# Reordering the first pairs of each feed-forward stage in a two-layer decoder step: the first seven-product pair's silu and product ahead of the plain pair's, and the copy of up and a weight split ahead of the last token group

## The reference

```python
def swiglu(h, w_gate, w_up, w_down):
    return (jax.nn.silu(h @ w_gate) * (h @ w_up)) @ w_down

for i in range(DEPTH):
    xp = xp + 0.5 * swiglu(rmsnorm(xp, ffn_norm[i, 0]), ffn_w_gate[i, 0], ffn_w_up[i, 0], ffn_w_down[i, 0])
    ...
    xp = xp + yp        # yp: sparse attention in layer 0, sliding window attention in layer 1
    ...
    xp = xp + 0.5 * swiglu(rmsnorm(xp, ffn_norm[i, 1]), ffn_w_gate[i, 1], ffn_w_up[i, 1], ffn_w_down[i, 1])
```

## Time and profile before

| | us |
|---|---|
| median of 3 runs | 2277.26 |
| lowest and highest | 2271.42, 2283.96 |
| time of the profiled execution | 2277.23 |
| its span, first to last instruction | 2275.4 |
| TensorE busy | 2154.5 |
| VectorE busy | 1334.2 |
| GpSimd busy | 1174.3 |
| ScalarE busy | 947.3 |

### The profile page before, as it was taken

How to read it: one execution, slowest core, us unless ns; L and a number is a source line. 1 busy time by engine, 2 the same in 40 slices (tenths; PEclk the granted TensorE clock), 3 DMA queues, 4 the chain that set the end, 5 groups by cost and what they waited for, 6 DMA issues and landing times.

```text
span 2275.4 us, 40915 instructions
## 1 busy us (share of the span) xinstructions
PE 2154.5 (95%) x15007; PEld 1969.7 (87%) x15007; DVE 1334.2 (59%) x2282; ACT 947.3 (42%) x1891; POOL 1174.3 (52%) x817
## 2 busy tenths in 40 slices
PE   7799999999989889899999899999999998999997
PEld 6799999958766578899999899999997698999997
DVE  5736455778885448637365753637556567455453
ACT  5425344341454325525255442525314435344343
POOL 4638576414201027748575775848641067666571
PEclk9899999999998999999999999999999898999998
DMA  5344453644203442444444252444461033535341
GB/s 129 71 114 106 121 112 93 118 80 121 41 2 101 123 103 56 90 87 91 87 93 93 66 102 65 97 91 91 96 152 31 1 75 67 111 69 117 66 103 42
DMA packets 378147, 197.68 MB, mean 87 GB/s; under 512 B 66531, under 2 KB 374476, under 8 KB 377932
## 3 DMA queue, kind: packets, MB, share of 16 engines
q1 hardware_dynamic: 366108, 180.79, 35.9%
q10 hardware_dynamic: 11552, 13.71, 2.0%
q0 software_dynamic: 288, 0.56, 0.1%
HBM read 192.23 MB, written 11.64 MB: 90 GB/s over the span
## 4 chain that ended last, share of the span: by engine, by line
PE 51%; DVE 6%; ACT 2%; issue 2%; POOL 2%; DVEq 0%; POOLq 0%; ACTq 0%
PE psum L1054 8%; PE psum L1055 8%; PE psum L1056 8%; PE psum L1013 7%; PE psum L1014 4%; PE psum L1016 4%; PE psum L1012 4%; PE psum L1015 3%; DVE squares L2495 1%; DVE psum L2347 1%; PE psum L1386 1%; PE psum L1416 1%; PE psum L1402 1%; PE psum L1382 1%; DVE XS L2336 1%
## 5 line engine op out<-in xcount | busy, mean ns | idle before, releaser
L802 POOL CAST WSP<-WST 128x1024 fp32r<-128x1024 f32 (+1 forms) x41 | 45.0, 1098 | 486.5 <-PE psum L1016 339.0
L835 POOL TENSOR_TENSOR WSP<-WST,WSP 128x512 fp32r<-128x512 f32 x106 | 153.4, 1451 | 151.3 <-ACT WSP L1739 151.2
L1054 PE MATMUL psum<-XT,WSP 128*128 128x288 f32 x656 | 199.2, 304 | 8.7 <-ACT back_up L1770 7.3
L1055 PE MATMUL psum<-XT,WSP 128*128 128x288 f32 x656 | 197.0, 300 | 0.0
L1056 PE MATMUL psum<-XT,WSP 128*128 128x288 f32 x656 | 196.2, 299 | 0.0
L1054 PE MATMUL psum<-XS,WSP 128*128 128x288 f32 x552 | 165.0, 299 | 15.9 <-DVE GS L2422 15.9
L2595 DVE SCALAR_TENSOR_TENSOR X<-psum,X 128x576 f32<-128x576 f32 x64 | 48.4, 756 | 213.6 <-PE psum L1016 213.6
L1056 PE MATMUL psum<-XS,WSP 128*128 128x288 f32 x552 | 163.5, 296 | 0.0
L1055 PE MATMUL psum<-XS,WSP 128*128 128x288 f32 x552 | 163.5, 296 | 0.0
L1013 PE MATMUL psum<-GS,WSP 128*128 128x512 f32 x406 | 161.5, 398 | 0.0
L2347 DVE SCALAR_TENSOR_TENSOR psum<-S,WST 128x512 f32<-128x512 f32 x70 | 107.2, 1531 | 86.3 <-POOL S L815 84.8
(11 more groups left out here) (450 smaller groups left out, 7454.6 us busy)
## 6 DMA issues: line engine op xcount, KB each, us to landing
WST<-in_ffn_w_gate SPq DMA_DIRECT2D x148, 256.0 KB, 4.8
WST<-in_ffn_w_down SPq DMA_DIRECT2D x144, 224.0 KB, 4.2
WST<-in_ffn_w_up SPq DMA_DIRECT2D x104, 256.0 KB, 4.1
WSTX<-in_ffn_w_up SPq DMA_DIRECT2D x64, 256.0 KB, 4.3
WSTX<-in_ffn_w_down SPq DMA_DIRECT2D x48, 224.0 KB, 4.2
WST<-in_a_w_in SPq DMA_DIRECT2D x28, 256.0 KB, 4.5
kv0A<-in_cache_kv SPq DMA_DIRECT2D x48, 128.0 KB, 2.3
kv2A<-in_cache_kv SPq DMA_DIRECT2D x48, 128.0 KB, 2.3
```

What stands on the lines that cost most here:

```text
L835: nc.gpsimd.tensor_tensor(by_pair(low), raw, by_pair(high).bitcast(F32), ALU.subtract).then_inc(pool_set, 1)
L1054: mm(out, high[:, c], operand(prod, 0, k), start=first and k == 0, stop=False, skip_group_check=True)
L1055: mm(out, high[:, c], operand(prod, 1, k), start=False, stop=False, skip_group_check=True)
```

## The change

On DVE and ACT the plain pair's last steps move behind the first seven-product pair's. In ffn1 to ffn3 that is: DVE runs the hidden chain of pair 1 and the gate of pair 2, then the plain pair's four operations, and only then `up_second(2)`. In ffn0 with its two plain pairs, plain pair 0 is finished after the gate of pair 3 and plain pair 1 after the gate of pair 4. The numbers that the semaphores count to follow (`hidden_before`). ACT's silus and high copies move alike.

At the head of ffn1 to ffn3, ACT copies the plain pair's up product (`up_copy`) before the high parts of the last token group's first sum and of P6's and P3's weights. POOL makes the low part of P5's weights before `last_sum(i, 2)` and P2's, and the tokens' low parts ahead of the sum S3. In ffn0, DVE takes the plain gate ahead of the last token sums.

```diff
+def hidden_before(name, p):
+
+    order = [PLAIN[name]]
+    for k in range(PLAIN[name]):
+        order += [k, PLAIN[name] + 1 + k]
+    return FFNS.index(name) * NF + (order.index(p) if p in order else p)
...
@@ GpSimd, start @@
+                if i:
+                    first_sum(i, 2)
+                    sum_up(name, p)
+                    low_of_raw(name, p, "P1")
+                    token_low(i, 2, 0)
+                    low_of_sum(name, p, "P5")
+                    last_sum(i, 2)
+                    low_of_raw(name, p, "P2")
+                    first_sum(i, 3)
+                    token_low(i, 2, 1)
+                    token_low(i, 3, 0)
+                    sum_first(name, p)
+                    last_sum(i, 3)
+                    token_low(i, 3, 1)
...
@@ TensorE, p1 @@
                 if p > 1 and plain(name, p - 2):
                     pe.wait_ge(gate_set, 2 * (n - 1))
+                elif p > 1:
+                    pe.wait_ge(hidden_set, 2 * (hidden_before(name, p - 2) + 1))
...
@@ ScalarE, update @@
                         scaled(6)
                         scaled(7)
+                        up_copy(to, PLAIN[to] - 1)
                         token_high(3, (0,))
                         high_of(to, PLAIN[to], "P6")
                         high_of(to, PLAIN[to], "P3")
-                        up_copy(to, PLAIN[to] - 1)
                         token_high(3, (1, 2, 3))
...
@@ ScalarE, ffn @@
+                    silu(name, p)
                     if q == 0:
-                        for k in range(p):
-                            silu(name, k)
-                    silu(name, p)
+                        silu(name, 0)
...
-                        if q == 0 and p == first + 1:
-                            for k in range(first):
-                                hidden_high(name, k)
                         hidden_high(name, p - 1)
                         next_high(p, "P2")
                         next_high(p, "P7")
                         silu(name, p)
                         next_high(p, "P4")
+                        if q == 0 and plain(name, p - first - 1):
+                            hidden_high(name, p - first - 1)
+                            if plain(name, p - first):
+                                silu(name, p - first)
...
@@ VectorE, load_x @@
+                plain_gate("ffn0", 0)
                 token_sums(0, 3)
-                plain_gate("ffn0", 0)
...
@@ VectorE, ffn @@
-                        if q == 0 and p == first + 1:
-                            for k in range(first):
-                                plain_up(name, k)
-                                plain_hidden(name, k)
-                                plain_low(name, k)
                         hidden(name, p - 1)
                         hidden_low(name, p - 1)
                         gate_second(name, p)
                         gate_first(name, p)
                         gate_scaled(name, p)
+                        if q == 0 and plain(name, p - first - 1):
+                            plain_up(name, p - first - 1)
+                            plain_hidden(name, p - first - 1)
```

More of the change, by code:

```diff
@@ L236, in count_pool @@
                 if follows_plain(name, p):
-                    keys += [(name, p, k) for k in ("S1", "P1", "P2", "P5", "S3", "P7")]
+                    keys += [(name, p, k) for k in (("S1", "P1", "P5", "P2") if FFNS.index(name) else ("S1", "P1", "P2", "P5"))]
+                    keys += [(name, p, k) for k in ("S3", "P7")]
                 else:
@@ L533, in plain_room @@
         def plain_room(half, p):
+            if half == "up_back" and p:
+                half, p = "gate_back", 0
             return plain_rooms[half, p][:, :]
@@ L921, in start @@
                     token_low(i, 1, 1)
[L922 to L938, removed]
+                if i:
[12 more added lines that the diff above has]
+                    token_low(i, 3, 1)
+                else:
+                    for k in range(KP):
+                        first_sum(i, k)
+                        token_low(i, k, 0)
+                        last_sum(i, k)
+                        if k < 2:
+                            low_of_plain(name, 1, halves_of_plain(1)[k])
+                        elif k == 2:
+                            sum_up(name, p)
+                            low_of_raw(name, p, "P1")
+                            low_of_raw(name, p, "P2")
+                            low_of_sum(name, p, "P5")
+                            sum_first(name, p)
+                        token_low(i, k, 1)
                 low_of_sum(name, p, "P7")
@@ L1945, in hidden_high @@
             def hidden_high(name, p):
-                act.wait_ge(hidden_set, 2 * pair_number(name, p) + 1)
+                act.wait_ge(hidden_set, 2 * hidden_before(name, p) + 1)
                 fn(GH[:, p % DB, :], plain_room("up", p) if plain(name, p) else bank_ab(name, p), ACT.Copy).then_inc(gh_set, 1)
@@ L2409, in hidden @@
             def hidden(name, p):
-                n, ab = pair_number(name, p), bank_ab(name, p)
+                n, ab = hidden_before(name, p), bank_ab(name, p)
                 dve.wait_ge(w_used, DONE[name, p, "P4"])
-                dve.wait_ge(up_sum, n + 1)
+                dve.wait_ge(up_sum, pair_number(name, p) + 1)
                 steps.done(stt(ab, ab, -1.0, rstd[:, :], ALU.mult, ALU.mult))
@@ L2418, in hidden_low @@
             def hidden_low(name, p):
-                n = pair_number(name, p)
+                n = hidden_before(name, p)
                 dve.wait_ge(gh_set, n + 1)
@@ L2441, in plain_hidden @@
             def plain_hidden(name, p):
-                n, u = pair_number(name, p), plain_room("up", p)
+                n, u = hidden_before(name, p), plain_room("up", p)
                 dve.wait_ge(silu_done, n + 1)
                 tt(u, u, plain_room("gate", p), ALU.mult).then_inc(hidden_set, 1)
-            def plain_low(name, p):
-                n, u = pair_number(name, p), plain_room("up", p)
                 dve.wait_ge(hidden_set, 2 * n + 1)
```

## The result

The changed kernel takes 2286.39 us (median of 20 runs, 2280.24 to 2292.83), the kernel before 2275.30 us in the same comparison (20 runs). The ratio is 1.0047, 95% interval 1.0036 to 1.0057: slower by 11 us. The interval does not hold 1, so the difference is real, but it lies just under the 0.5% that the prediction took as the line between no change and slower. The profiled execution's span is 2285.2 us against 2275.4.

The account below looks back on a forecast made before the run. PE bounds the kernel, busy 95% of the span, the rest its waits. 3 x (2.7 + 0.4) for ffn1 to ffn3 plus 2.9 for ffn0 gives +12.2, 2289.5 us; own range 2283 to 2296, overall 2272 to 2300.

Parts of the forecast that it names:

- The exchange of stalls: ffn1: P1(3)'s wait mostly goes; P5(3) waits 5 to 7 us for `up_second`, with clock 0.50 behind it.
- the step: Tail, ffn1: hidden chain and P1(3) start 4.30 us earlier; plain operations meet POOL's backlog of four, P5(3) at 927.45.
- rival (c): POOL's backlog holds DVE 5.54 us, so P1(4) waits too; head takes its full bound: 2294 us, chance 0.12.
- The blocked port: Tail, ffn1: the plain pair's DVE operations are held beside POOL's, 1.3 to 2 us each; P5(3) at 927.4.
- Rival (a): Tail: DVE's later three plain operations are not held beside POOL; P5(3) at 924.5, sum -2.6, 2274.6 us, chance 0.20.
- The row that carried the estimate: L2347, a two-input DVE operation right behind a POOL operation: 0.69 us at least, 1.78 in the middle, 5.54 at worst.
- for the tail: Plain pair behind pair 1 in ffn1: P6(3) at 932.66 instead of 929.94, costing 2.7 us.
- the head's term: Head of ffn1: the wait moves from P5(1) to P6(1), 3.5 us; costs 0.4, bounds -0.1 and +1.0.
- 5.21 - 3.75: From P5(3) to P6(3): P5 and P4 take 3.16 us plus 2.05 for the slow clock.
- +2.9: ffn0: -0.4 - 0.8 + 6.1 - 2.05, from its head and two plain-pair insertions, with a new stall at P5(5).
- The head's term there: ffn0: earlier plain gate gains PE about 2 us at P1(2); waits for copies and weights leave a gain of 0.4.
- Rival (b): Clock stays at 2.4 GHz through new stalls at P6(1) and P5(3): -15.3, 2274.2 us ports blocked, 2259 free; chance 0.12.

Follow-up runs that it names:

- the tail part alone: Changed kernel with GpSimd's order, `up_copy` and ffn0's plain gate put back, leaving only the plain pair's later finish: 2284.05 us, 1.0043 of the kernel before.
- the head part alone: Kernel before with only GpSimd's order, `up_copy` and ffn0's plain gate as in the changed kernel: 2273.90 us, 1.0000 of the kernel before.
- the last experiment: Kernel before plus plain pair ahead of weight sums, its high copies later, new heads, and P1's product copy before P7's high part: 2256.36 us, 0.9922.
- the kernel with GpSimd held: Changed kernel, with GpSimd also waiting before P2's weights' low part until the plain pair's values are finished: 2277.09 us, 1.0013 of the kernel before.

## Why the prediction came out as it did

**The exchange of stalls held.** P1(3)'s wait went from 5.83 to 1.51 and P5(3) waits 6.21 behind `up_second`, with the clock at 0.50. P1(3) came 4.20 us earlier where 4.30 was the step (4.33 in the tail part alone, in ffn1), and from P1(3) to P5(3) it was 8.05 us against the 8.6 that was worked out. P1(4) did not wait, so rival (c), a further wait, fell. (Its sum was off as well: 3 x (0.8 + 0.6) is 4.2, not 4.5, which still ends at 2294.)

**The blocked port held, and decides.** Rival (a), a free port, asks for P5(3) at most 5.65 us behind P1(3). With GpSimd idle it is 5.46; with GpSimd beside it, as in the change, 8.05. The row that carried the estimate, L2347, was a fair guide: 0.69 to 1.78 there, 0.76 to 1.71 here. The Trainium skill, "SBUF — State Buffer", section "Who interferes with whom", says that a VectorE instruction with two SBUF inputs and a GpSimd instruction that reads SBUF contend. The trace agrees for the three plain operations that met one, 1.12, 1.71 and 1.70 us in place of 0.41, 0.76 and 0.76. The fourth took 0.76: GpSimd's backlog had run out by then, as the step had counted.

**In ffn1 the sum came out by two errors that cancel.** Up to P5(3) the prediction has 1.26 (927.45 - 926.19) for the tail and 0.4 for the head, +1.66 in each of three stages; measured were +0.81, +0.76 and +0.69, that is 2.7 us less in all. 0.55 us of it a stage lie between P1(3) and P5(3): the first plain operation started 1.45 us behind P1(3) instead of 1.67, and from there to `up_second` it was 6.09 instead of 6.43. The rest is the head's term and the little by which P1(3) was early. Behind P5(3) the prediction has 5.21 - 3.75 = 1.46 us in all three stages. From P5(3) to P6(3) it was 5.93 us in ffn1, 5.18 in ffn2 and 4.54 in ffn3, and before, that stretch took 3.75, 4.32 and 3.37. So the difference is 2.18, 0.86 and 1.17, which is 4.2 in all against 4.4: right in the sum and in no single stage. ffn1's +3.08 against 3.1 is 0.85 too little before P5(3) and 0.72 too much behind it, and that is luck. ffn1 was copied to the other two stages on the strength of a like pattern of waits; the clock behind them was not alike. The three stages cost 6.6 us instead of 9.3, nearly all of it before P5(3), and that is most of the gap between the forecast of 12.2 and the 9.8 of the profiled spans. The medians differ by 11.1, with an interval of about 8 to 13, which holds both 9.8 and 12.2.

**The head.** Its term of +0.4 is nothing that can be measured: the head part alone gives 1.0000 [0.9991, 1.0009]. The wait moved to P6(1), as said, and was 3.42 against 3.5. Its releaser was another one. In the changed kernel, ScalarE's timeline shows

```profile
901.28 0.61 ACT L1767 ACTIVATE WSP<-S 128x512 fp32r<-128x512 f32 x1
901.80 0.39 ACT L1950 ACTIVATE shots<-psum 128x288 f32<-128x288 f32 x1
```

and GpSimd's low part, which the prediction named, is done before:

```profile
900.86 0.80 POOL L890 TENSOR_TENSOR XT<-tsum,XT 128x288 fp32r<-128x288 f32 x1
```

It ends at 901.66, ScalarE's copy at 902.19, and P6(1) starts at 902.25. P6(1) also needs ScalarE's copy of P1's product, which the list of waits ahead of the prediction leaves out too. That copy's place behind L1767 makes half a microsecond of the wait: with it ahead of L1767 in the last experiment, the stall was 2.96.

**ffn0.** +2.8 measured against +2.9, with stalls at P5(4) and, new, at P5(5), 5.64 us behind P1(5) against 5.7. The head's term there had the wrong sign: it was a gain of 0.4, but counted from the end of the plain part, P1(4) starts at 27.39 us in the changed kernel and at 27.01 in the tail part alone. What P1(2) gains by its 2.37 us goes into longer waits for ScalarE's copies, 1.47 us at P6(2), where there was none, and 1.85 at P6(3), where there was 0.72.

**The clock does not stay up.** Rival (b) fell for the long stalls: 0.50 to 0.65 in the stretches behind the stalls of about 6 us, and 0.50 over 4.4 us behind the 3.61 at P5(3) of the kernel with GpSimd held. For stalls of 3.4 us it is true in some stages and not in others; the last section has the numbers. Most of (b)'s chance stood under faster, though with the port blocked its own time, 2274.2, is no change.

What stays open: the kernel with GpSimd held has 10.4 us less of waits behind `up_second`, and its ratio is 0.0034, about 8 us, better than the changed kernel's. The two ratios are to different sets of runs, and each interval reaches about 2.5 us to either side, so the two figures do not contradict each other, and the contention's price in the median is known no more closely. The spread of single runs of the changed kernel, 2280 to 2293, is as wide as the effect. The longer ones tend to have the lower mean granted clock: the correlation is -0.63 over its 20 runs, and between -0.41 and -0.82 in each set of runs of the experiments. Which stalls lower the clock in one run and not in another was not tested.

## What to carry to other kernels

Work that is moved out from under one wait in an in-order queue lands on the next: list for each engine it runs on who stands behind it now and when that one is needed, ScalarE's hop included. Look for the place by the moved engine's own idle time ahead of the critical point (here 4.50 us in front of the sums, worth 0.7%), not by which of two results is needed first. And price a VectorE operation with two inputs in SBUF by whether GpSimd runs beside it in the new place; the duration in the old place (0.76 here, against 1.71) does not say that.

## What the runs showed that I had not expected

A stall of 3.4 us of PE goes either way. Of the three stalls at P6(1) in the changed kernel, behind 3.40 us in ffn2 the granted clock stayed at 1.00, behind 3.42 in ffn1 it was 0.61 over 4.4 us, and in ffn3, behind 3.41, it was 0.54 over 3.2 us; the three stages run the same instructions there. The trace of the head part alone has it the other way round, with ffn1 at full clock (stretches at P6(1) in ffn1 and ffn2, behind 3.42 and 3.33 us):

```profile
896.60:900.00 3.40, 3.40 (x26) 3.40 (x27) 2.76 (x6) 2.29 (x5) 3.40 (x3) 1.00 0.00 0
1284.50:1288.00 3.50, 3.46 (x14) 3.46 (x15) 2.86 (x6) 1.50 (x4) 3.50 (x3) 0.50 0.00 0
```

In about 3.4 us PE ran 26 matmuls at the one and 14 at the other. The length of the stall alone doesn't tell the two apart, so one profiled execution doesn't tell what such a stall costs in the median. The duration of the first matmul behind the stall (0.40 or 0.61) is no sign either: it was 0.40 in ffn3 of the changed kernel, with the clock at 0.54 behind it.

GpSimd pays for the contention too: beside the first two held VectorE operations its own next ones, L826 and L846, took 1.44 and 1.77 us instead of 1.28. And the engines do not always take turns one for one. The 5.54 us of the earlier trace rows are in ffn0 of the kernel before, from 108.74 to 114.28: GpSimd ran L835 twice, L844 and L826 back to back until 113.72, and only then did the one VectorE operation come through.
